# State-space decay matrices: from triangle products on TensorE to broadcast row sums on ScalarE

## The reference, cut to what matters

```
acs   = cumsum(a)                                # per head, over the 128 tokens of a chunk
seg   = acs[i] - acs[j]
decay = exp(where(i >= j, seg, -inf))            # a 128x128 matrix per head, chunk and direction
y     = (C_i . B_j) * decay @ xdt                # within the chunk
y    += (C @ h_in) * exp(acs)                    # from the state that enters the chunk
```

## Time and profile before

| | before |
|---|---|
| median of 3 runs, us | 1224.19 (1223.82 to 1225.85) |
| span of the profiled execution, us | 1221.5 |
| PE, DVE, ACT, POOL busy in the span, us | 1171.0, 712.2, 492.5, 27.3 |
| loop over eight steps, by the timeline, us from the span's start | 866.8 to 904.5 |

### The profile page before, as it was taken

The page is one execution under the profiler, slowest core; times in us unless marked ns, Lnnn a source line. Parts: engine busy times, 40 slices in busy tenths (PEclk is TensorE's granted clock), DMA queues, the critical chain, the costliest instruction groups (busy, mean ns, idle before and its releaser), DMA issues.

```text
span 1221.5 us, 18383 instructions
## 1 busy us (share of the span) xinstructions
PE 1171.0 (96%) x7498; PEld 954.3 (78%) x7498; DVE 712.2 (58%) x1185; ACT 492.5 (40%) x741; POOL 27.3 (2%) x31
## 2 busy tenths in 40 slices
PE   4999999999999999999999999999889999999998
PEld 3777776677688888888887668898446798999998
DVE  3499988743542334323333378977979645556544
ACT  4343235742443332222222433455148736554442
POOL 0100000000000000000000000001500000000000
PEclk9999999999999999999999999999999999999999
DMA  9745355016553222433224553434214157546632
GB/s 359 250 153 192 130 177 178 1 61 216 172 173 104 86 69 86 135 106 104 64 63 148 198 185 116 126 108 153 78 44 139 36 173 256 193 133 216 203 111 96
DMA packets 124333, 170.72 MB, mean 140 GB/s; under 512 B 4797, under 2 KB 112743, under 8 KB 120039
## 3 DMA queue, kind: packets, MB, share of 16 engines
q1 hardware_dynamic: 121430, 164.99, 40.3%
q10 hardware_dynamic: 2833, 4.74, 1.3%
HBM read 168.63 MB, written 1.08 MB: 139 GB/s over the span
## 4 chain that ended last, share of the span: by engine, by line
PE 85%; DVE 10%; ACT 2%; issue 2%; DMA 1%; ACTq 0%; SPq 0%; POOL 0%; DVEq 0%
PE acc L1923 22%; PE acc L1924 22%; PE acc L1925 22%; PE pmod L1862 2%; PE acc L1985 1%; PE p L1810 1%; PE acc L1987 1%; PE acc L1986 1%; PE acc L2517 1%; PE p L2543 1%; DVE seg L1714 1%; PE acc L1810 1%; DMA xin<-in_ctx 1%; PE p L2146 1%; DVE sm L1352 1%
## 5 line engine op out<-in xcount | busy, mean ns | idle before, releaser
L555 DVE TENSOR_TENSOR w_lo<-raw,w_hi 128x1024 fp32r<-128x1024 f32 x234 | 259.0, 1148 | 247.6 <-ACT w_hi L545 247.3
L545 ACT ACTIVATE w_hi<-raw 128x1024 fp32r<-128x1024 f32 (+1 forms) x236 | 221.6, 987 | 436.2 <-PE acc L1925 407.0
L1923 PE MATMUL acc<-Hhi,w_hi 128*128 128x512 f32 (+1 forms) x976 | 334.7, 343 | 6.9 <-POOL ptap L624 4.5
L1925 PE MATMUL acc<-Hhi,w_lo 128*128 128x512 f32 (+1 forms) x976 | 332.2, 340 | 0.0
L1924 PE MATMUL acc<-Hlo,w_hi 128*128 128x512 f32 (+1 forms) x976 | 332.1, 340 | 0.0
L1923 PEld LDWEIGHTS acc<-Hhi,w_hi 128*128 128x128 f32 x976 | 186.5, 191 | 32.2 <-issue 9.0
L1925 PEld LDWEIGHTS acc<-Hhi,w_lo 128*128 128x128 f32 x976 | 186.4, 191 | 20.4
L1924 PEld LDWEIGHTS acc<-Hlo,w_hi 128*128 128x128 f32 x976 | 186.5, 191 | 19.9
L1923 PE MATMUL acc<-hid_hi,w_hi 128*128 128x512 f32 (+1 forms) x448 | 157.3, 351 | 0.0
L1924 PE MATMUL acc<-hid_lo,w_hi 128*128 128x512 f32 (+1 forms) x448 | 155.7, 348 | 0.0
L1925 PE MATMUL acc<-hid_hi,w_lo 128*128 128x512 f32 (+1 forms) x448 | 155.7, 348 | 0.0
(11 more groups left out here) (328 smaller groups left out, 1393.3 us busy)
## 6 DMA issues: line engine op xcount, KB each, us to landing
raw<-in_mod_w SPq DMA_DIRECT2D x48, 1024.0 KB, 5.3
raw<-in_ffn_w_in SPq DMA_DIRECT2D x44, 1024.0 KB, 5.1
raw<-in_od_w_in SPq DMA_DIRECT2D x15, 1024.0 KB, 5.3
raw<-in_ffn_w_out SPq DMA_DIRECT2D x16, 768.0 KB, 4.2
raw<-in_ev_w_in SPq DMA_DIRECT2D x10, 1024.0 KB, 7.6
raw<-in_ffn_w_out SPq DMA_DIRECT2D x16, 640.0 KB, 3.8
raw<-in_od_w_out SPq DMA_DIRECT2D x8, 1024.0 KB, 4.9
raw<-in_ev_w_out SPq DMA_DIRECT2D x8, 768.0 KB, 6.0
```

The source lines that it names most:

```text
L545: nc.scalar.activation(w_hi[:, w % 2, c0:c1], raw[:, r % RAW_SLOTS, c0:c1], ACT.Copy)\
L555: nc.vector.tensor_tensor(w_lo[:, w % 2, c0:c1], raw[:, r % RAW_SLOTS, c0:c1], w_hi[:, w % 2, c0:c1].bitcast(F32), ALU.subtract).then_inc( ...
L1923: mm(outs[m], hi[:, j, cols], xh, start=(first and j == 0), stop=False)
L1925: ins = mm(outs[m], lo[:, j, cols], xh, start=False, stop=(last and j == kts - 1))
```

## The change

The loop no longer makes seg by a product of triangles. The cumulative sums are stored as rows beside their exponentials, and loaded with a broadcast to all 128 partitions; the same sums stand as a column in `cum`, from four more entries of `CUM`. ACT computes Relu(column - row), which is zero outside the allowed side where the difference would have the wrong sign, for one head at a time (128x128, the column as bias), four instructions per q, and then one exponential of the negative over 128x512 per q. The exponential of q-1 is issued behind the Relus of q. The decay matrices have six buffers, the masking multiply is in place in them. All row loads move from ACT's queue to SP's, in one order written out before the load of the second output block.

```diff
-        row_exp = X[0:16, 6:8, LAT:T]
-        row_store = nc.dram_tensor("row_store", (4, 16, P), F32).ap()
-        CD = [XC[:, 8, :], XC[:, 9, :]] + [Cd[:, i, :] for i in range(4)]
+        cum = view("cum", [2 * LT, 16], r_xc + 22528 + 512)
+        row_sums, row_exp = X[0:16, 4:6, LAT:T], X[0:16, 6:8, LAT:T]
+        row_store = nc.dram_tensor("row_store", (2, 4, 16, P), F32).ap()
@@ stream of loads, buffers
         stream += [("mod", 1, 2, k) for k in range(4)]
+        ROWS_AT = len(stream)
         stream += od_out_blocks[1:]
-        rx = view("rx", [4, 512], r_split + idle)
+        row_early = view("row_early", [4, 512], r_split + idle)
         seg = view("seg", [4, 512], r_split + 16384 + idle)
+        CD = [XC[:, 8, :], XC[:, 9, :]] + [row_late[:, i, :] for i in range(4)]
+        DECAY = ([heads4(seg[:, i, :]) for i in range(4)]
+                 + [X[:, 4 * i:4 * i + 4, LAT + P:T] for i in range(2)])
@@ SP
+            def row_load(to, which, q, name):
+                (b, c), d = SEG[q // 2], q % 2
+                sp.dma_start(to, row_store[which, 2 * c + d, 4 * b:4 * b + 4, :].rearrange("h i -> (h i)")
+                             .partition_broadcast(P)).then_inc(s(name), 16)
+            def sums_load(q):
+                row_load(row_early[:, q % 4, :], 0, q, f"sums_loaded{q % 4}")
+            def factors_load(q):
+                row_load(CD[q % 6], 1, q, f"cd_loaded{q % 6}")
             while r < FF[1][0]:
+                if r == ROWS_AT:
+                    sp.wait_ge(s("row_stored"), 64)
+                    sp.wait_ge(block_done, C_OUT)
+                    for q in range(4):
+                        sums_load(q)
+                    sp.wait_ge(s("cb_mm"), 1)
+                    factors_load(0)
+                    factors_load(1)
+                    sp.wait_ge(s("xw_used"), 6)
+                    for q in range(2, 6):
+                        factors_load(q)
+                    for k in range(2, 8):
+                        for q in (2 * k, 2 * k + 1):
+                            sp.wait_ge(s("sums_read"), q - 3)
+                            sums_load(q)
+                        if k < 7:
+                            sp.wait_ge(s("inter_mm"), k - 1)
+                            factors_load(2 * k + 2)
+                            factors_load(2 * k + 3)
                 load(r)
@@ POOL
-            for k, (b, c) in enumerate(SEG):
-                ...
-                    nc.gpsimd.tensor_tensor(rx[:, (2 * k + d) % 4, :] ..., ALU.mult).then_inc(s("rx_ready"), 1)
@@ ACT, turn n=10 of the input stage
+                        A(row_sums, p5[0:16, :].rearrange("p (a n) -> p a n", a=2), ACT.Copy)
                         A(row_exp, p5[0:16, :].rearrange("p (a n) -> p a n", a=2), ACT.Exp).then_inc(s("row_exp_ready"), 1)
+                        A(cum[:, :, :], pmod[:, 128:192].rearrange("p (n h) -> p n h", n=4), ACT.Copy)
                         ...
-                        for c in range(2):
-                            act.dma_start(row_store[2 * c:2 * c + 2, :, :] ...)
+                        for which, rows_ in enumerate((row_sums, row_exp)):
+                            for c in range(2):
+                                act.dma_start(row_store[which, 2 * c:2 * c + 2, :, :] ...)
@@ ACT, state-space stage
+            def decay(q):
+                if q < 16:
+                    (b, c), d = SEG[q // 2], q % 2
+                    act.wait_ge(s(f"sums_loaded{q % 4}"), 16 * (q // 4 + 1))
+                    if q >= 6:
+                        act.wait_ge(s("intra_mm"), q // 2 - 2)
+                    for h in range(4):
+                        ins = A(DECAY[q % 6][:, h, :], row_early[:, q % 4, h * P:(h + 1) * P], ACT.Relu, scale=-1.0,
+                                bias=cum[:, 2 * c + d, 4 * b + h:4 * b + h + 1])
+                    ins.then_inc(s("sums_read"), 1)
+                if q:
+                    act.wait_ge(s("sums_read"), q)
+                    A(DECAY[(q - 1) % 6], DECAY[(q - 1) % 6], ACT.Exp, scale=-1.0).then_inc(s("decay_ready"), 1)
-            for k in range(8):
-                act.wait_ge(s("seg_mm"), k + 1)
-                ...
-                A(seg[:, (2 * k + 1) % 4, :], RB[k % 3][:, :], ACT.Exp).then_inc(s("decay_ready"), 1)
-                if 1 <= k < 6:
-                    act.wait_ge(s("inter_mm"), k)
-                    ...
-                        rows_out(q)
-                if k % 2 == 1 and k > 1:
+            state_copy(0)
+            state_copy(1)
+            for q in range(4):
+                decay(q)
+            state_copy(2)
+            state_copy(3)
+            for k in range(2, 8):
+                for d in range(2):
+                    decay(2 * k + d)
+                if k == 7:
+                    decay(16)
+                if k % 2 == 1:
                     square_y(k // 2 - 1)
@@ DVE
+                    dve.wait_ge(s("row_stored"), 64)
                     V_.tensor_copy(qrowC[:, 0:P], p7[0:16, 0:P])
...
             for k, (b, c) in enumerate(SEG):
-                dve.wait_ge(s("decay_ready"), k + 1)
-                both_ways = heads4(seg[:, (2 * k + 1) % 4, :])
                 for d in range(2):
-                    if d:
-                        dve.wait_ge(s("m_ready"), 2 * k + 1)
-                    V_.tensor_tensor(heads4(seg[:, (2 * k + d) % 4, :]), both_ways,
+                    q = 2 * k + d
+                    dve.wait_ge(s("decay_ready"), q + 1)
+                    V_.tensor_tensor(DECAY[q % 6], DECAY[q % 6],
                                      CB[...], ALU.mult).then_inc(s("m_ready"), 1)
@@ PE
-            def decays(k):
-                ...
-                for d in range(2):
-                    pe.wait_ge(s("rx_ready"), 2 * k + d + 1)
-                    ins = mm(RB[k % 3][:, :], cst(("after", "before")[d]), rx[:, (2 * k + d) % 4, :], ...)
-                ins.then_inc(s("seg_mm"), 1)
                 ins.then_inc(s("intra_mm"), 1)
-                if k + 3 < 8:
-                    decays(k + 3)
+                if k == 0:
+                    pe.wait_ge(s("state_act"), 4)
+                    pe.wait_ge(s("state_dve"), 2)
@@ CUM
     (("after", 0, 0),), (("before", 1, 1),),
+    (("upto", 0, 0),), (("from", 0, 1),), (("upto", 1, 0),), (("from", 1, 1),),
```

More of the change, by code:

```diff
@@ L267, in build_trunk @@
         XW = view("XW", [2, S_INNER], r_big + 16384)
-        Cd = view("Cd", [4, 512], r_big + 16384)
+        row_late = view("row_late", [4, 512], r_big + 16384)
         Dcol = view("Dcol", [KD], region(32))
@@ L568, in build_trunk @@
         OUT_BANK = ((p5, p6), (p7, pmod))
-        RB = (p5, p6, p7)
         def xs_half(k):
@@ L1659, in _ @@
             dve.wait_ge(s("cb_mm"), 1)
-            dve.wait_ge(s("row_stored"), 32)
             pcb = pmod[:, :].rearrange("p (n i) -> p n i", n=4)
@@ L2454, in _ @@
                 ins.then_inc(s("xw_used"), 1)
-            def decays(k):
-                if k >= 3:
-                    pe.wait_ge(s("decay_ready"), k - 2)
-                for d in range(2):
-                    pe.wait_ge(s("rx_ready"), 2 * k + d + 1)
-                    ins = mm(RB[k % 3][:, :], cst(("after", "before")[d]), rx[:, (2 * k + d) % 4, :], start=(d == 0),
-                             stop=(d == 1))
-                ins.then_inc(s("seg_mm"), 1)
             def sum_y(b):
@@ L2471, in sum_y @@
                         .then_inc(s("ssy_mm"), 1)
-            pe.wait_ge(s("state_act"), 4)
-            decays(0)
-            decays(1)
-            pe.wait_ge(s("state_dve"), 2)
-            decays(2)
+            pe.wait_ge(s("state_act"), 2)
             for k, (b, c) in enumerate(SEG):
```

34 lines of the change are left out of this document (6 added, 28 removed).

## The result

| | before | changed |
|---|---|---|
| median, us | 1224.01 (4 runs, 1223.31 to 1225.85) | 1233.02 (4 runs, 1232.41 to 1235.34) |
| span of the profiled execution, us | 1221.5 | 1230.6 |
| DVE, PE, POOL busy, us | 712.2, 1171.0, 27.3 | 703.2, 1163.3, 7.5 |
| loop: DVE's entry to the end of the last gating, us | 866.81 to 904.45 | 865.08 to 913.32 |

The account below looks back on a forecast made before the run. The prediction took DVE to bound the loop, as long as the others feed it. Loop tie +1.0, column sums +0.4 and late ACT +1.5 gave +2.9 on 1221.5: span 1224.4, median 1227.1, range 1218.3 to 1232.5 us.

Parts of the forecast that it names:

- landing of the third load in such a burst: 4.6: Loop: the first sums load, behind two factor loads, lands 4.6 us after its issue, within a 10.05 us path.
- E(0): Loop: end of PE's state products of step 0, forecast at 869.2 to 869.3 us.
- E(6): Loop: end of PE's state products of step 6, forecast at 899.45 us.
- my 30.15: Loop: forecast time for three two-step links, steps 0 to 6, each put at 10.05 us.
- My first rival: Loop: PE's granted clock falls, or a crowded DMA queue costs alike; +3.5 us beyond forecast, 1230.6; chance 0.22.
- my sum: Whole kernel: forecast terms added, +2.9 us on the span, giving a median of 1227.1 us.
- The tie: Loop: sums loads wait behind factor loads and inter_mm, 10.05 us per two steps; loop ends 1.0 us later.
- E(k-2): Loop: end of PE's state products two steps earlier, which SP awaits before issuing factors, then sums.
- POOL's silence: Loop: sixteen POOL instructions go, freeing 8.5 us of DVE, 1.0 of it before the loop.
- The input stage: Before the loop: extra column sums on PE cost +0.4 us, late ACT copies and stores +1.5.
- rival 3: ACT in the loop: Relu needs its own table, two loads per q, 41 us partly hidden; 1255 or more; chance 0.02.
- The rival of the faster side: Loop: sums land in time, path below 8.4 us, only POOL's silence remains; priced at 1219.5; chance 0.24.

Follow-up runs that it names:

- e2: Changed kernel without the ten factor loads of q = 6 to 15 (output not the reference's): 1223.11 us, ratio 0.9996.
- e4: Changed kernel with two triangle products per step put back on PE as idle work in steps 0 to 6: 1231.27 us, ratio 1.0059.
- e13: Changed kernel with the two halves of row_store in HBM swapped, exponentials first and sums second: 1233.72 us, ratio 1.0081.
- e18: Changed kernel with the loop's ten factor loads issued by POOL and the sums loads waiting only for their buffer: 1227.96 us, ratio 1.0037.
- e5: Kernel before with its 16 factor loads moved from ACT's queue to SP's, same order and waits: 1220.93 us, ratio 0.9978.
- e6: Kernel before with factor loads on SP, plus twelve unread 256 KB loads in pieces of 512 B: 1221.09 us, ratio 0.9979.
- e7: Kernel before with twelve of POOL's sixteen triangles left out (output not the reference's): 1219.22 us, ratio 0.9968.
- e9: Kernel before with factor loads on SP, plus twelve unread 256 KB loads in pieces of 2 KB: 1221.37 us, ratio 0.9980.
- e16: Changed kernel with the loop's ten factor loads issued by ACT and the sums loads waiting only for their buffer: 1223.02 us, ratio 1.0000.
- e11: Changed kernel with sixteen copies of the stored rows in HBM, the eight wider stores issued by POOL: 1233.95 us, ratio 1.0076.
- e15: Changed kernel with the loop's ten factor loads issued by ACT behind its Relus, sums still waiting for inter_mm on SP: 1226.82 us, ratio 1.0030.
- e17: Changed kernel with the loop's ten factor loads issued by POOL, sums still waiting for inter_mm on SP: 1230.39 us, ratio 1.0053.
- e1: Changed kernel with SP issuing the next step's sums ahead of the inter_mm wait and the factor loads: 1228.11 us, ratio 1.0033.

## Why the prediction was wrong

1. **The landing: the step that failed.** I put "landing of the third load in such a burst: 4.6", from the earlier trace rows. It is 7.31, 6.57 and 7.27, so 7.4 us over three links, of the 8.0 by which the way from E(0) to E(6) exceeds my 30.15. e2 takes it away and the time with it. My first rival had named a crowded queue, but "four loads per step, 4.9 each", which is still 2.4 us short of what was measured. A better term stood in the trace of before. The pairs of the loop took 4.3 at a rate near 170 GB/s; two more loads of 0.26 MB at that rate are 3.1 us, less 0.86 for the later issue: 6.5. With it my sum would have been 5.8 us higher, 1232.9. That it meets the result so closely is in part luck, since other terms were off and cancel (points 3 to 5), and since the rate near 170 GB/s is itself unexplained. I took the median of the one burst that held the slice of 351 GB/s and met an empty queue, and did not ask at what rate such loads run in the loop, or whether the burst before would have landed.
2. **The tie** from E(k-2) over factors, sums, Relus and mask to E(k) was right, with its two interlaced paths and with DVE waiting ahead of every second mask. Four Relus take 1.28 (forecast 1.08), the exponential 0.61 (0.60), the mask 0.69 (0.7).
3. **The clock**, my first rival, came on top. I held against it that "no gap of over 2 us arises"; PE idled for 4.04 ahead of 865.92, and the granted clock was 0.72 in 866 to 872. The state products then took 1.92 and not 1.26, in the first link though not in the next two. By e4 it is 1.3 to 1.7 us, where the rival had 3.5 beyond the forecast.
4. **POOL's silence** brought what I said on DVE: masks at 0.69, and DVE in the loop 1.7 us earlier, of which 0.6 had come about before the stage began; 1.1 is left, where I had 1.0. It could not help in the loop, where loads set the pace.
5. **The input stage** cost nothing where I had +1.9. ACT there in the changed kernel, the four stores and the split, to be held against the earlier trace rows:

```profile
812.78 1.77 ACTq L993 DMA_DIRECT2D row_store<-X  x4
814.65 2.01 ACT L580 ACTIVATE w_hi<-raw 128x1024 fp32r<-128x1024 f32 x2 [1.64 <-issue]
```

   Four stores were issued in less time than two before (1.95), and the split came 0.3 earlier than its old time. A store's issue of 1.57 did not occur again. PE left the stage 0.6 us earlier than before, but that says nothing: DVE's copy `Btok<-p` right behind it starts at 847.44 in the changed kernel and at 847.1 to 849.1 in e2, e4 and e13 to e18, which have the same instructions up to there, and at 847.6 to 848.3 in the kernel before, e5, e6, e7 and e9. Within that spread the input stage cost nothing.
6. **Relu's table.** From the first Relu to the end of the loop there is one table load, at 855.53, ahead of the first exponential and behind eight Relus, so rival 3 is refuted. The Trainium skill, "ScalarE: Activation LUTs", section "Table sets", has Relu in every set; the trace agrees.

The books: DVE enters the loop 1.7 earlier and takes 48.2 us for it in place of 37.6, which is +8.9 at the loop's end; the span is +9.1. Of the loop's 10.6, 7.4 are landings above forecast and 1.9 the tie as forecast (39.55 for 37.64). In the first step DVE's entry to E(0) took 4.2 and not 3.4, 0.8 more, with the granted clock at 0.72; 0.5 is left for the rest of the clock, the Relus and SP's issues.

The rival of the faster side needed landings below those forecast; it failed on the same term. The rule that I had cited from the Trainium skill, "DMA: Bandwidth & Descriptors", section "Anatomy of one DMA", 2.0 us plus the bytes at 436 GB/s, gives an estimate of 2.6 for such a load. The page measured loads issued by GpSimd, and the traces do not agree: the loads landed in 4.3 in pairs, in 7.3 in the changed kernel's bursts, and in 8.3 to 11.2 from POOL's queue beside others.

Open: why row loads run at 120 to 185 GB/s in most slices of the loop, and at 290 to 380 in single slices of every kernel. e9 and e16 show the high rate more often than the changed kernel, e9 with about as many loads of the same kind, e16 with the very loads of the change. Source, piece, place and destination have been varied one at a time. The copies of the source took 0.8 us off the landing (e11), the others nothing. What e9 and e16 have in most of the loop and the changed kernel has not is distance between the loads; it does not explain the first six loads, and no run varies it alone. A busy PE is not it, by e4.

## What to carry to other kernels

Before you hang a step on a load, read the rate that such loads get in the slices of that stretch and add up the bytes that are under way together, instead of taking the landing of the fastest burst: here it grew from 4.3 with two loads to 7.3 with four, where each burst met the rest of the one before, and POOL's queue did not help (7.6). When a critical load and a mere refill become due at one event, issue the critical one and hold the refill back for some us (6.2 of the 9.0 us came back in e15, which also moved the refill to ACT's queue). And try first to give the work of the engine that disturbs the pace to an engine with idle time, without any load: POOL's triangles on ACT won 6.5 us, with another 2.5 for loads that no longer stand in ACT's stream.

## What the runs showed of the hardware

- A load of one 2 KB row to 128 partitions (256 KB in SBUF) moved at 120 to 185 GB/s in most slices of 1.2 us, with single slices of 290 to 380, in kernels with and without the change. Stretches of six us reached 241 (e6) and 270 (e16).
- Two queues gave little or no more than one over the loop (866 to 902): 176 GB/s in e15 and 167 in e17, beside 168 in the changed kernel; with sums first, 175 in e16 (two queues) and 184 in e1 (one).
- Eight stores with sixteen copies each held ACT's queue for 8.45 us; four plain ones took 1.77.
- Loads issued by POOL landed in 8.3 to 11.2 us in the median, beside 7.6 for SP's in the same bursts; each pair of issues held POOL for 1.07 to 1.22 us.
- ACT's Relu of 128x128 with a pointer as bias takes 0.39 us; four in a row take 1.26 to 1.28, so they start 0.29 to 0.30 apart.
